# A two-layer hybrid with mixtures of experts on one core: all 32 experts loaded by index, all weight loads on one queue, no rank tables in the routing

## The chip, the cores and the metric

The kernel runs on one core of one Trainium2 chip. The metric is the device time of one execution in microseconds (us). A kernel's time is the median over runs. A profiled execution is shown with its own span.

## What is computed

Two layers over 1024 latent tokens (a batch of one, width 1024) and 256 context tokens. Layer 0 mixes with gated DeltaNet heads and a short convolution, layer 1 with windowed attention; after each comes a hierarchical mixture of experts. Layer 0's mixture works on all 1280 tokens, layer 1's on the 1024 latent ones. Everything is float32. The change touches the mixture only:

```python
def hier_moe(x, w_group, w_expert, w1, w3, w2):
    g_sel = argmax(x @ w_group)                   # one group of 4
    e_in = (x @ w_expert)[g_sel]                  # 8 experts of that group
    top_p, top_i = top_k(softmax(e_in), 2)
    weights = p_group * top_p / sum(top_p)
    expert_id = g_sel * 8 + top_i
    return expert_ffn_sorted(x, expert_id, weights, w1, w3, w2)

# assignments sorted by expert; every block of rows with its own expert's weights
    h = silu(xb @ w1[e]) * (xb @ w3[e])
    return h @ w2[e]
```

An expert has w1 and w3 (1024 x 512) and w2 (512 x 1024), 2048 KB (2.1 MB) each.

## The kernel before

The program is a row of stages, each a block in which all five engines run their own instruction stream and wait for each other by semaphores. A block ends when every engine has ended; then the next begins. The mixture `moe` is: a norm with the router's logits, `route`, `experts`, `combine`.

**`route`** runs on VectorE, instruction after instruction, each waiting for the one before. It counts tokens by expert and rounds each expert up to units of 64 rows. An assignment's row among them is its slot. GpSimd then writes the tokens' numbers to their slots by indirect DMAs (L1172). After the slots, VectorE goes on with a table: active experts in rank order (EXPERT), how many blocks are needed up to the last row of each rank (BLOCKS_UPTO), and for each block of 128 rows (two units) in which of the three buffers the weights of its two units lie, how many loads each buffer must have had by then, and which loads to make next (NEXT). The last instruction casts the table to integers (L1329). In layer 0 the same block also computes the modulation of layer 1 (`modulation`, its rows by VectorE at L232), which has no part in the mixture.

**`experts`** runs over the blocks of 128 rows. `w13` and `w2` are rings of three buffers, one expert each (RING = 3). TensorE does for block j, in this order: the transposes of the x of block j + 1 (L1439), those of the h of block j - 1 (L1445), up(j), which is 64 matmuls with w1 and w3 (L1463), and down(j - 1), which is 32 matmuls with w2 (L1483). ACT and VectorE copy and apply silu between them. GpSimd gathers the rows of x by an indirect DMA (L1412), ACT stores y (L1531).

The weights are loaded by two issuers:
- SP (`load13`, L1382) loads w1 and w3 of the next rank as soon as the buffer is free: w1 after the w1 half of up of the last block that used the buffer, w3 after its w3 half.
- ACT (`refill`, L1534 to L1549, then `load2`, L1538) issues w2 loads after it has copied and stored the y of a block: it reads from the table which ranks' buffers that block has freed.

up(j) waits for the loads into each w13 buffer that the table asks for, so for all experts up to its own second unit's; down(j) waits likewise for w2.

What the given inputs route follows from the reference alone. In layer 0 there are 56 units in 28 blocks, and their experts are (0,1) (2,3) (4,5) (6,7) (8,8) (9,10) (11,12) (12,13) (14,15) (16,17) (17,17) (17,17) (17,18) (18,18) (18,18) (19,19) (19,20) (20,21) (21,21) (22,22) (23,23) (23,23) (23,24) (24,25) (26,27) (28,28) (29,29) (30,31). In layer 1 there are 49 units in 25 blocks: (0,1) (2,2) (3,4) (4,5) (5,5) (5,5) (6,6) (6,7) (7,8) (9,10) (11,12) (13,14) (14,15) (15,16) (16,17) (17,18) (18,19) (20,20) (21,22) (23,24) (24,25) (25,26) (27,28) (29,30) (31,31). All 32 experts have tokens in both layers. Blocks are numbered from 0.

Of the kernel before, what the change touches and what calls it, by code (L numbers as in the profile page):

```python
# [21 lines left out]
P = 128  # L22
# [20 lines left out]
MAXP = ((2 * TOK + NE * (UNIT - 1)) // UNIT + 1) // 2  # L43
# [91 lines left out]
def ds(i, n):  # L135
    return bass.ds(i, n)
# [968 lines left out]
class Table:  # L1105


    BLOCKS, LAST, ACTIVE = 0, 1, 2
    EXPERT = 3
    BLOCKS_UPTO = EXPERT + NE  # L1110
    OF_BLOCK = BLOCKS_UPTO + NE
    PER = 2 + RING + 3
    NEXT = 2 + RING


    SIZE = OF_BLOCK + PER * (MAXP + 1)


def route(k, first, logits, slots, wts, table):
# [20 lines left out]
    active, rank_upto, rank = k.sb("active", [P, NE]), k.sb("active_upto", [P, NE]), k.sb("active_before", [P, NE])  # L1140
    far, last = k.sb("units_upto_if_active", [P, NE]), k.sb("last_rank", [P, 1])
    cmp, owner = k.sb("compare", [P, U, NE]), k.sb("owner_rank", [P, U])
    triple, rounds = k.sb("multiples_of_ring", [P, NE // RING + 1]), k.sb("rounds", [P, RING, U])
    last_unit, thresholds2 = k.sb("units_upto_rank", [P, NE]), k.sb("even_numbers", [P, MAXP])
    blocks_of = k.sb("blocks_of", [P, NE, MAXP])
    nxt = k.sb("next_rank", [P, MAXP + 1])
# [45 lines left out]
    def _(dve):  # L1192
# [59 lines left out]
        st.link(V.tensor_reduce(units[:], over[:], AX.X, ALU.add))  # L1252
        st.link(V.tensor_tensor_scan(incl[:], ones[:, 0:NE], units[:], 0.0, ALU.mult, ALU.add))
# [5 lines left out]
        for c in range(2):  # L1259
# [9 lines left out]
        R = slice(0, NE)  # L1269
        by_rank = ramp[:, R].unsqueeze(2).to_broadcast([P, NE, NE])  # L1270
        st.link(V.tensor_tensor(cmp[:, R], rank_upto[:].unsqueeze(1).to_broadcast([P, NE, NE]), by_rank, ALU.is_le))
        st.link(V.tensor_reduce(tf[:, Table.EXPERT:Table.EXPERT + NE], cmp[:, R], AX.X, ALU.add))
        st.link(V.tensor_scalar(tf[:, Table.EXPERT:Table.EXPERT + NE], tf[:, Table.EXPERT:Table.EXPERT + NE],
                                float(NE - 1), None, ALU.min))
        st.link(V.tensor_tensor(cmp[:, R], rank[:].unsqueeze(1).to_broadcast([P, NE, NE]), by_rank, ALU.is_le))
        st.link(V.tensor_tensor(cmp[:, R], cmp[:, R], units[:].unsqueeze(1).to_broadcast([P, NE, NE]), ALU.mult))
# [8 lines left out]
        st.link(V.tensor_copy(tf[:, Table.ACTIVE:Table.ACTIVE + 1], rank_upto[:, NE - 1:NE]))  # L1285

        st.link(V.tensor_scalar(far[:], active[:], -float(2 * U), float(2 * U), ALU.mult, ALU.add))
        st.link(V.tensor_tensor(far[:], far[:], incl[:], ALU.add))
        st.link(V.tensor_tensor(cmp[:], far[:].unsqueeze(1).to_broadcast([P, U, NE]),
                                ramp[:, 0:U].unsqueeze(2).to_broadcast([P, U, NE]), ALU.is_le))  # L1290
# [24 lines left out]
        st.link(V.tensor_scalar(last[:], rank_upto[:, NE - 1:NE], -float(RING), None, ALU.add))  # L1315
        st.link(V.tensor_scalar(last[:], last[:], 0.0, None, ALU.max))
        st.link(V.tensor_scalar(nxt[:], nxt[:], last[:, 0:1], None, ALU.min))
        st.link(V.tensor_scalar(per[:, :, Table.NEXT], nxt[:], float(RING), None, ALU.add))
        for u in range(2):

            if u:
                st.link(V.tensor_scalar(nxt[:], nxt[:], 1.0, None, ALU.add))
            st.link(V.tensor_scalar(triple[:], ramp[:, 1:NR + 1], float(RING), None, ALU.mult))
            st.link(V.tensor_tensor(cmp[:, 0:B, 0:NR], nxt[:].unsqueeze(2).to_broadcast([P, B, NR]),
                                    triple[:].unsqueeze(1).to_broadcast([P, B, NR]), ALU.is_ge))
            st.link(V.tensor_reduce(rounds[:, 0, 0:B], cmp[:, 0:B, 0:NR], AX.X, ALU.add))
            st.link(V.scalar_tensor_tensor(out=per[:, :, Table.NEXT + 1 + u], in0=rounds[:, 0, 0:B], scalar=-float(RING),
                                           in1=nxt[:], op0=ALU.mult, op1=ALU.add))
# [8 lines left out]
def experts(k, l, first, table):  # L1337
# [31 lines left out]
    @block.sync  # L1369
    def _(sp):  # L1370
        def entry(base, m, lo, hi):
            return sp.value_load(table[0:1, ds(m + base, 1)], min_val=lo, max_val=hi)

        def load13(m, r, wait=True):
            e = entry(Table.EXPERT, m, 0, NE - 1)
            used = entry(Table.BLOCKS_UPTO, m - RING, 1, MAXP) if wait else None

            for half, name in enumerate(("moe_w1", "moe_w3")):
                if wait:

                    sp.wait_ge((xw1_ready, up_ready)[half], primed(used))
                sp.dma_start(w13[:, r, half, :], dr[name][l, ds(e, 1)].rearrange("a (p j) n -> p (a j n)", p=P)).then_inc(w13_in[r], 16)  # L1382

        active = sp.value_load(table[0:1, Table.ACTIVE:Table.ACTIVE + 1], min_val=1, max_val=NE)
# [123 lines left out]
    @block.scalar  # L1508
    def _(act):
        def first(j):  # L1510

            act.wait_ge(xw1_ready, primed(j + 1))
            if not isinstance(j, int):
                act.wait_ge(h_turned, primed(j))
            nc.scalar.activation(h[:], k.bank[UP[0]][:], ACT.Silu).then_inc(silu_ready, 1)
            turned(j + 1)

        def turned(j):
            act.wait_ge(x_turned, primed(j + 1))
# [12 lines left out]

        def value(column, lo, hi):
            return act.value_load(table[0:1, ds(column, 1)], min_val=lo, max_val=hi)  # L1534

        def load2(rank, r):
            e = value(rank + Table.EXPERT, 0, NE - 1)
            act.dma_start(w2[:, r, :], dr["moe_w2"][l, ds(e, 1)].rearrange("a (p j) n -> p (a j n)", p=P)).then_inc(w2_in[r], 16)  # L1538
# [650 lines left out]
```

## Time and profile before

| | us |
|---|---|
| median of 3 runs | 4399.15 |
| lowest and highest run | 4390.29, 4408.07 |
| span of the profiled execution | 4404.1 |
| TensorE busy in the span | 3422.2 |
| first up to the last down of `experts`, layer 0 | 1755.8 to 2489.1 |
| the same, layer 1 | 3702.3 to 4338.9 |

The profiled execution is 5 us above the median. All times in rows are counted from the start of its span. Of TensorE's rows, PE is the matmuls and PEld the loads of the stationary operand. "q" behind an engine is its instruction sequencer, which waits, branches and issues DMAs. "<-" in brackets names what ended an engine's idle time.

### The profile page before, as it was taken

What the parts mean: (1) busy time and instruction counts of PE and PEld (TensorE: products, weight loads), DVE (VectorE), ACT (ScalarE), POOL (GpSimd) and SP (SyncE); (2) the same over time, 40 slices, a digit from 0 to 9 for tenths busy, and PEclk for the clock granted to TensorE, in tenths of its full rate; (3) what the DMA queues carried; (4) which work ended last, traced back from release to release, by engine and by line L of the source; (5) the groups of instructions that cost most, each with busy time, mean ns of one, the idle gap of its engine ahead of it and who ended that gap; (6) DMA issues with size and microseconds to landing.
All of it is one profiled execution on the core that took longest, in us unless ns stands there. A gap on an engine that the chain in (4) does not pass through costs nothing. (4 is left out here: it accounts for less than half of the span.)

```text
span 4404.1 us, 48676 instructions
## 1 busy us (share of the span) xinstructions
PE 3422.2 (78%) x15274; PEld 1825.7 (41%) x15275; DVE 1381.0 (31%) x2407; ACT 638.0 (14%) x1396; POOL 582.0 (13%) x522
## 2 busy tenths in 40 slices
PE   4899997999886952889998567677777953999983
PEld 0644443888883430233333133344444431333331
DVE  2223322555555162000111341155556142111014
ACT  1112211000002020000000121133334010000002
POOL 0000000333331111000000212111111111000002
PEclk7799998999997965899999778877778966999996
DMA  7311101011101067997567520120100017779994
GB/s 298 121 48 48 46 26 60 25 39 39 39 20 48 0 202 254 395 405 311 189 240 307 203 93 25 42 98 18 35 17 18 10 50 288 275 314 378 381 384 181
DMA packets 148767, 657.50 MB, mean 149 GB/s; under 512 B 25441, under 2 KB 63105, under 8 KB 117921
## 3 DMA queue, kind: packets, MB, share of 16 engines
q1 hardware_dynamic: 110688, 421.45, 25.3%
q10 hardware_dynamic: 17040, 162.24, 9.1%
q0 software_dynamic: 20912, 72.13, 4.7%
q8 instruction: 79, 1.29, 0.1%
q14 instruction: 48, 0.39, 0.0%
HBM read 586.41 MB, written 69.36 MB: 149 GB/s over the span
## 5 line engine op out<-in xcount | busy, mean ns | idle before, releaser
L1463 PE MATMUL bank<-w,xT 128*64 x3392 | 761.2, 608 | 52.6 <-DMA w<-in_moe_w 47.0
L502 PE MATMUL bank<-aT,w 128*128 128x512 f32 (+1 forms) x1344 | 500.7, 535 | 6.7 <-DVE short L661 5.9
L1463 PEld LDWEIGHTS bank<-w,xT 128*64 128x64 f32 x3392 | 244.9, 140 | 530.1 <-issue 525.4
L1483 PE MATMUL bank<-w,hT 128*64 (+1 forms) x1696 | 388.3, 611 | 64.6 <-issue 37.4
L502 PEld LDWEIGHTS bank<-aT,w 128*128 128x128 f32 x1344 | 266.4, 199 | 236.2 <-issue 220.0
L1580 DVE TENSOR_TENSOR h<-h,bank 128x512 f32<-128x512 f32 x53 | 36.5, 688 | 816.7 <-PE bank L1463 816.7
L1483 PEld LDWEIGHTS bank<-w,hT 128*64 128x64 f32 x1696 | 130.0, 140 | 321.7 <-issue 317.3
L1776 PE MATMUL bank<-at_w_in,aT 128*128 128x512 f32 x416 | 190.7, 620 | 3.5 <-PEq L116 3.5
L1439 PE MATMUL bank<-eye,x 128*128 128x128 f32 x440 | 65.5, 295 | 154.6 <-DMA x<-moe_x,idx_block 130.8
L377 PE MATMUL bank<-eye,a 128*128 128x128 f32 x304 | 68.1, 408 | 142.6 <-DVE a L361 132.1
L1975 PE MATMUL bank<-probsT,v_win 128*64 128x256 f32 x384 | 149.2, 566 | 36.4 <-DVE probsT L2077 36.4
L1961 PE MATMUL bank<-eye,probs 128*128 128x128 f32 x640 | 110.2, 314 | 72.2 <-POOL probs L2026 58.7
L1412 POOL DMA_INDIRECT x<-moe_x,idx_block x55 | 53.1, 965 | 853.1 <-PE bank L1439 851.4
L931 PE MATMUL bank<-T,AT 128*128 128x128 f32 x960 | 143.2, 301 | 12.3 <-DVE T L881 12.3
L2026 POOL TENSOR_TENSOR probs<-probs,den 128x640 f32<-128x640 f32 x64 | 80.3, 1254 | 498.2 <-DVE den L2060 498.2
L203 PE MATMUL bank<-ada_w,silu_c 128*2 128x512 f32 x384 | 78.4, 912 | 79.6 <-DMA ada_w<-in_ada_w 78.1
L1439 PEld LDWEIGHTS bank<-eye,x 128*128 128x128 f32 x440 | 55.7, 196 | 201.2 <-DMA x<-moe_x,idx_block 134.1
L931 PEld LDWEIGHTS bank<-T,AT 128*128 128x128 f32 x960 | 128.5, 209 | 23.2 <-DVE T L881 16.1
L931 PE MATMUL bank<-TT,A_T_off 128*128 128x128 f32 x960 | 126.7, 276 | 0.0
L1776 PEld LDWEIGHTS bank<-at_w_in,aT 128*128 128x128 f32 x416 | 82.8, 201 | 105.8 <-issue 105.8
L1961 PEld LDWEIGHTS bank<-eye,probs 128*128 128x128 f32 x640 | 78.6, 157 | 113.1 <-issue 84.1
L377 PEld LDWEIGHTS bank<-eye,a 128*128 128x128 f32 x304 | 58.0, 217 | 153.7 <-issue 115.3
(317 smaller groups left out, 4422.4 us busy)
## 6 DMA issues: line engine op xcount, KB each, us to landing
w<-in_moe_w SPq DMA_DIRECT2D x128, 2048.0 KB, 15.9
w<-in_moe_w ACTq DMA_DIRECT2D x64, 2048.0 KB
ada_w<-in_ada_w SPq DMA_DIRECT2D x48, 1024.0 KB, 22.4
moe_y<-y ACTq DMA_DIRECT2D x53, 512.0 KB
w<-in_ab_w_in SPq DMA_DIRECT2D x28, 512.0 KB, 3.7
moe_x<-a SPq DMA_DIRECT2D x18, 512.0 KB
moe_y<-zero POOLq DMA_DIRECT2D x1, 8192.0 KB, 26.2
at_w_in<-in_at_w_in SPq DMA_DIRECT2D x3, 2048.0 KB, 17.0
```

The lines of the kernel that those rows point to most:

```text
L203: mm = pe.matmul(bank(g, q)[32 * q:32 * q + 2, :], sc[:, j, :], w[:, j, q * NW:(q + 1) * NW], start=(j == 0), stop=(j == KC - 1))
L377: t = pe.transpose(k.bank[2 * u + c // 4][:, (c % 4) * P:(c % 4 + 1) * P], a[u][:, c * P:(c + 1) * P], k.eye[:])
L502: mm = pe.matmul(k.bank[3 * s + n][:, 0:width], w[j][:, c, :], aT[:, c, at:at + width], start=(c == 0), stop=(c == KC - 1))
L931: mm = pe.matmul(to[:, h, :], lhs[:, h, :], rhs[:, h, :], start=start, stop=stop)
L1412: pool.indirect_dma_start(x[:], None, dr["moe_x"], bass.IndirectOffsetOnAxis(ap=one[:, 0:1], axis=0)).then_inc(x_in, 16)
L1439: t = pe.transpose(k.bank[X[c // 4]][:, (c % 4) * P:(c % 4 + 1) * P], x[:, c:D:KC], k.eye[:])
L1463: mm = pe.matmul(k.bank[UP[half]][u * UNIT:(u + 1) * UNIT, :], xT[:, c, u * UNIT:(u + 1) * UNIT], w13[:, r if u else ds(buf[0], 1), half, ...
L1483: mm = pe.matmul(k.bank[Y[half]][u * UNIT:(u + 1) * UNIT, :], hT[:, c, u * UNIT:(u + 1) * UNIT], w2[:, r if u else ds(buf[0], 1), at:at + ...
L1776: mm = pe.matmul(k.bank[3 * s + g][:], aT[:, c, t * P:(t + 1) * P], w[:, c, g * 512:(g + 1) * 512], start=(c == 0), stop=(c == KC - 1))
L1961: mm = pe.transpose(k.bank[6 + f % 2][:, at:at + P], pr[m % 2][:, h, c * P:(c + 1) * P], k.eye[:])
L1975: mm = pe.matmul(to[HD * h:HD * h + HD, 0:2 * P], v, pt[g % 2][:, c, h, :, :], start=(c == 0), stop=(c == 4))
L2026: nc.gpsimd.tensor_tensor(pr[m % 2][:, 0, :], pr[m % 2][:, 0, :], small[m % 2]["den"][:, 0:1].to_broadcast([P, W + C]), ALU.mult).then_inc ...
```

## The change

The table loses the rank columns: EXPERT, ACTIVE and the three NEXT columns. Ranks are now the experts' own indices, and every expert gets at least one unit, with or without tokens (`ALU.max` with 1.0). SP loads all 32 experts in a written-out order, with w2 one place behind w1 and w3, and waits for the freed buffer by an entry of BLOCKS_UPTO. ACT loads no weights any more. MAXP is 36 with either formula.

```diff
-MAXP = ((2 * TOK + NE * (UNIT - 1)) // UNIT + 1) // 2
+MAXP = ((2 * TOK + NE * UNIT) // UNIT + 1) // 2
...
+def expert_at(n):
+    return n
...
         st.link(V.tensor_reduce(units[:], over[:], AX.X, ALU.add))
+        st.link(V.tensor_scalar(units[:], units[:], 1.0, None, ALU.max))
...
-        st.link(V.tensor_scalar(active[:], units[:], 1.0, None, ALU.min))
-        st.link(V.tensor_tensor_scan(rank_upto[:], ones[:, 0:NE], active[:], 0.0, ALU.mult, ALU.add))
-        st.link(V.tensor_tensor(rank[:], rank_upto[:], active[:], ALU.subtract))
...
-        st.link(V.tensor_reduce(last_unit[:], cmp[:, R], AX.X, ALU.add))
         st.link(V.tensor_scalar(thresholds2[:], ramp[:, 0:MAXP], 2.0, None, ALU.mult))
-        st.link(V.tensor_tensor(blocks_of[:], last_unit[:].unsqueeze(2).to_broadcast([P, NE, MAXP]),
+        st.link(V.tensor_tensor(blocks_of[:], incl[:].unsqueeze(2).to_broadcast([P, NE, MAXP]),
                                 thresholds2[:].unsqueeze(1).to_broadcast([P, NE, MAXP]), ALU.is_gt))
...
-        B = MAXP + 1
-        st.link(V.tensor_tensor(cmp[:, 0:B], tf[:, Table.BLOCKS_UPTO:Table.BLOCKS_UPTO + NE].unsqueeze(1).to_broadcast([P, B, NE]),
-                                ramp[:, 0:B].unsqueeze(2).to_broadcast([P, B, NE]), ALU.is_le))
-        st.link(V.tensor_reduce(nxt[:], cmp[:, 0:B], AX.X, ALU.add))
...
         st.link(V.tensor_copy(table[:], tf[:]))
...
     @block.sync
     def _(sp):
-        def entry(base, m, lo, hi):
-            return sp.value_load(table[0:1, ds(m + base, 1)], min_val=lo, max_val=hi)
-
-        def load13(m, r, wait=True):
-            e = entry(Table.EXPERT, m, 0, NE - 1)
-            used = entry(Table.BLOCKS_UPTO, m - RING, 1, MAXP) if wait else None
-
+        def used_upto(m):
+            at = Table.BLOCKS_UPTO + m
+            return sp.value_load(table[0:1, at:at + 1], min_val=1, max_val=MAXP)
+
+        def load13(m):
+            r, e = m % RING, expert_at(m)
+            used = used_upto(m - RING) if m >= RING else None
             for half, name in enumerate(("moe_w1", "moe_w3")):
-                if wait:
+                if m >= RING:
 
                     sp.wait_ge((xw1_ready, up_ready)[half], primed(used))
...
+        def load2(m):
+            if m >= RING:
+
+                sp.wait_ge(y_mm, primed(used_upto(m - RING)))
+            sp.dma_start(w2[:, m % RING, :], dr["moe_w2"][l, expert_at(m)].rearrange("(p j) n -> p (j n)", p=P)).then_inc(w2_in[m % RING], 16)
 
         sp.wait_ge(idx_in, 16)
-        load13(0, 0, wait=False)
+        load13(0)
         sp.wait_ge(x_in, 16)
-        for m in range(1, RING):
-            with sp.If(active > m):
-                load13(m, m, wait=False)
-        with sp.Fori(1, NE // RING + 1) as i:
-            for r in RR:
-                with sp.If(i * RING + r < active):
-                    load13(i * RING + r, r)
+        for m in range(1, NE):
+            load13(m)
+            load2(m - 1)
+        load2(NE - 1)
...
-        def refill(j):
-
-
-            per = j * Table.PER + Table.OF_BLOCK
-            lo, hi = value(per + Table.NEXT, RING, NE), value(per + (Table.PER + Table.NEXT), RING, NE)
-            for u in R2:
-                with act.If(lo + u < hi):
-                    buf = value(per + (Table.NEXT + 1 + u), 0, RING - 1)
-                    for r in RR:
-                        with act.If(buf == r):
-                            load2(lo + u, r)
-
-        active = value(Table.ACTIVE, 1, NE)
-        act.wait_ge(x_in, 16)
-        for m in RR:
-            with act.If(active > m):
-                load2(m, m)
         turned(0)
         first(0)
 
         def body(j):
             first(j)
             second(j - 1)
-            refill(j - 1)
```

The first place is SP's stream in the expert stage of layer 0. In the rows before, w_361 is `w13`; these are the first three experts and one turn of the loop over the ring:

```order
L1382 DMA w_361<-in_moe_w 128x4096 x2
L1390 COMPARE_AND_BRANCH
L1372 TENSOR_LOAD table
L1372 ISA x2
L1382 ISA
L1382 DMA w_361<-in_moe_w 128x4096 x2
...
L1394 COMPARE_AND_BRANCH
L1372 ISA
L1372 TENSOR_LOAD table
L1372 ISA x3
L1372 TENSOR_LOAD table
L1372 ISA x2
L1381 REGISTER_ALU
L1382 ISA
L1382 DMA w_361<-in_moe_w 128x4096 x2
```

In the changed kernel w_354 is `w13` and w_355 is `w2`; the stream starts so:

```order
L1346 DMA w_354<-in_moe_w 128x4096 x4
L1352 DMA w_355<-in_moe_w 128x4096
L1346 DMA w_354<-in_moe_w 128x4096 x2
L1352 DMA w_355<-in_moe_w 128x4096
L1337 TENSOR_LOAD table
L1337 ISA x2
L1345 REGISTER_ALU
L1346 DMA w_354<-in_moe_w 128x4096 x2
L1352 DMA w_355<-in_moe_w 128x4096
```

Each pair of w1 and w3 is now followed by one w2 in the same stream, and the branches are gone.

The second place is ACT's loop over the blocks. Before, the store of y is followed by table loads, branches and up to two loads of w2 (w_362):

```order
L1528 COPY y<-bank 128x512
L1531 ISA
L1531 DMA moe_y<-y 128x1024
L1534 ISA
L1534 TENSOR_LOAD table
L1534 ISA x3
L1534 TENSOR_LOAD table
L1534 ISA x2
L1546 COMPARE_AND_BRANCH
```

In the changed kernel the loop's body ends with the store:

```order
L1484 REGISTER_ALU
L1487 COPY xT<-bank 128x512
L1492 ISA
L1493 COPY y<-bank 128x512
L1496 ISA
L1496 DMA moe_y<-y 128x1024
```

## Rows read from the trace of the kernel before

**Rows 1.** The page: the span, and the busy time of each engine.

```profile
span 4404.1 us, 48676 instructions
...
PE 3422.2 (78%) x15274; PEld 1825.7 (41%) x15275; DVE 1381.0 (31%) x2407; ACT 638.0 (14%) x1396; POOL 582.0 (13%) x522
```

**Rows 2.** The page's costliest groups: the products up (L1463) and down (L1483).

```profile
L1463 PE MATMUL bank<-w,xT 128*64 x3392 | 761.2, 608 | 52.6 <-DMA w<-in_moe_w 47.0
...
L1483 PE MATMUL bank<-w,hT 128*64 (+1 forms) x1696 | 388.3, 611 | 64.6 <-issue 37.4
```

**Rows 3.** Windows: stretch, busy of each engine, then PEclk, DMA share, GB/s.

```profile
1755.00:2010.00 255.00, 211.40 (x940) 75.42 (x940) 23.36 (x35) 15.34 (x26) 10.30 (x18) 0.91 0.98 404
...
2010.00:2371.00 361.00, 341.15 (x1620) 124.41 (x1620) 39.40 (x59) 26.55 (x45) 16.22 (x29) 0.99 0.59 225
...
3712.00:3722.00 10.00, 7.62 (x41) 3.16 (x36) 1.98 (x3) 0.59 (x1) 0.60 (x2) 1.00 1.01 428
...
3702.00:3915.00 213.00, 199.86 (x942) 76.20 (x944) 22.66 (x34) 15.34 (x26) 9.37 (x17) 0.98 0.74 287
...
3915.00:3999.00 84.00, 71.76 (x320) 26.46 (x321) 8.02 (x12) 5.31 (x9) 3.44 (x6) 0.94 1.01 428
...
3999.00:4245.00 246.00, 228.76 (x1090) 85.36 (x1091) 27.41 (x41) 17.70 (x30) 12.44 (x21) 0.99 0.93 371
```

**Rows 4.** Timeline, TensorE, layer 0: start, length, what, idle time before.

```profile
1755.77 16.18 PE L1463 MATMUL bank<-w,xT 128*64 x64 [5.13 <-DMA w<-in_moe_w]
...
1782.15 16.64 PE L1463 MATMUL bank<-w,xT 128*64 x64 [7.03 <-DMA w<-in_moe_w]
...
1860.73 7.09 PE L1483 MATMUL bank<-w,hT 128*64 x32 [0.82 <-issue]
...
1867.89 1.13 PE L1439 MATMUL bank<-eye,x 128*128 128x128 f32 x8
...
1868.85 0.65 PE L1445 MATMUL bank<-eye,h 128*128 128x128 f32 x4
...
2010.01 13.95 PE L1463 MATMUL bank<-w,xT 128*64 x64 [2.07 <-DMA w<-in_moe_w]
...
2063.31 13.95 PE L1463 MATMUL bank<-w,xT 128*64 x64
...
2086.51 13.95 PE L1463 MATMUL bank<-w,xT 128*64 x64
```

**Rows 5.** Timeline, GpSimd, layer 0: waits for the first two gathers.

```profile
1729.63 0.18 POOL L1406 COPY idx_block<-idx 128x1 int32<-128x1 int32 x1 [10.95 <-DMA x<-moe_x,idx_block]
...
1748.79 0.18 POOL L1406 COPY idx_block<-idx 128x1 int32 x1 [15.38 <-DMA x<-moe_x,idx_block]
```

**Rows 6.** Timeline, ACT, layer 0: the copy of y and the next w2.

```profile
1836.90 0.59 ACT L1528 COPY y<-bank 128x512 f32<-128x512 f32 x1 [6.55 <-PE bank L1483]
...
1841.12 2.34 ACTq L1538 DMA_DIRECT2D w<-in_moe_w  x2
```

**Rows 7.** Timeline, VectorE, routing of layer 1.

```profile
3620.15 0.17 DVE L1265 TENSOR_SCALAR active<-units 128x32 f32<-128x32 f32 x1
...
3627.35 0.18 DVE L1278 TENSOR_SCALAR even_numbers<-ramp 128x36 f32<-128x36 f32 x1
...
3645.39 1.39 DVE L1312 TENSOR_TENSOR compare<-table_f,ramp 128x1184 f32<-128x1184 f32 x1
...
3652.74 0.35 DVE L1329 CAST table<-table_f 128x363 int32<-128x363 f32 x1
```

**Rows 8.** One line, L90, same stretch: the ends of the engines' blocks.

```profile
L90 POOLq DRAIN  x1: 1456/1456/1456, 3648.5 to 3648.5; - x1
```

**Rows 9.** Timeline, VectorE, layer 0: the routing's last row, the modulation's last.

```profile
1662.57 0.35 DVE L1329 CAST table<-table_f 128x363 int32<-128x363 f32 x1
...
1697.86 2.84 DVE L232 TENSOR_TENSOR rows<-bank,bias 2x512 f32<-2x512 f32 x4 [17.33 <-PE bank L203]
```

**Rows 10.** One tile, w, 1755 to 2010: durations min/median/max in ns.

```profile
L1463 PE MATMUL bank<-w,xT x576: 592/592/1116, 1755.8 to 1997.5; 128*64 x96, 128*64 128x512 f32 x96
```

More of the change, by code:

```diff
@@ L1105 @@
 class Table:
-    BLOCKS, LAST, ACTIVE = 0, 1, 2
-    EXPERT = 3
-    BLOCKS_UPTO = EXPERT + NE
+    BLOCKS, LAST = 0, 1
+    BLOCKS_UPTO = 2
     OF_BLOCK = BLOCKS_UPTO + NE
-    PER = 2 + RING + 3
-    NEXT = 2 + RING
+    PER = 2 + RING
     SIZE = OF_BLOCK + PER * (MAXP + 1)
+def expert_at(n):
+    return n
 def route(k, first, logits, slots, wts, table):
@@ L1139, in route @@
     over, thresholds = k.sb("over", [P, NE, MOST]), k.sb("thresholds", [P, MOST])
-    active, rank_upto, rank = k.sb("active", [P, NE]), k.sb("active_upto", [P, NE]), k.sb("active_before", [P, NE])
-    far, last = k.sb("units_upto_if_active", [P, NE]), k.sb("last_rank", [P, 1])
     cmp, owner = k.sb("compare", [P, U, NE]), k.sb("owner_rank", [P, U])
     triple, rounds = k.sb("multiples_of_ring", [P, NE // RING + 1]), k.sb("rounds", [P, RING, U])
-    last_unit, thresholds2 = k.sb("units_upto_rank", [P, NE]), k.sb("even_numbers", [P, MAXP])
+    thresholds2 = k.sb("even_numbers", [P, MAXP])
     blocks_of = k.sb("blocks_of", [P, NE, MAXP])
-    nxt = k.sb("next_rank", [P, MAXP + 1])
     ratio, inv = k.sb("ratio", [P, T]), k.sb("inv", [P, T])
@@ L1284, in _ @@
         st.link(V.tensor_scalar(tf[:, Table.LAST:Table.LAST + 1], tf[:, Table.BLOCKS:Table.BLOCKS + 1], -1.0, None, ALU.add))
[L1285 to L1289, printed above, removed]
+        st.link(V.tensor_tensor(cmp[:], incl[:].unsqueeze(1).to_broadcast([P, U, NE]),
                                 ramp[:, 0:U].unsqueeze(2).to_broadcast([P, U, NE]), ALU.is_le))
         st.link(V.tensor_reduce(owner[:], cmp[:], AX.X, ALU.add))
-        st.link(V.tensor_scalar(last[:], rank_upto[:, NE - 1:NE], -1.0, None, ALU.add))
-        st.link(V.tensor_scalar(owner[:], owner[:], last[:, 0:1], None, ALU.min))
+        st.link(V.tensor_scalar(owner[:], owner[:], float(NE - 1), None, ALU.min))
         NR = NE // RING + 1
@@ L1309, in _ @@
             st.link(V.tensor_copy(per[:, :, 2 + r], rounds[:, r, 1:U:2]))
-        B = MAXP + 1
-        st.link(V.tensor_tensor(cmp[:, 0:B], tf[:, Table.BLOCKS_UPTO:Table.BLOCKS_UPTO + NE].unsqueeze(1).to_broadcast([P, B, NE]),
-                                ramp[:, 0:B].unsqueeze(2).to_broadcast([P, B, NE]), ALU.is_le))
-        st.link(V.tensor_reduce(nxt[:], cmp[:, 0:B], AX.X, ALU.add))
[L1315 to L1328, printed above, removed]
         st.link(V.tensor_copy(table[:], tf[:]))
@@ L1370, in _ @@
     def _(sp):
-        def entry(base, m, lo, hi):
-            return sp.value_load(table[0:1, ds(m + base, 1)], min_val=lo, max_val=hi)
-        def load13(m, r, wait=True):
-            e = entry(Table.EXPERT, m, 0, NE - 1)
-            used = entry(Table.BLOCKS_UPTO, m - RING, 1, MAXP) if wait else None
+        def used_upto(m):
[4 more added lines that the diff above has]
+            used = used_upto(m - RING) if m >= RING else None
             for half, name in enumerate(("moe_w1", "moe_w3")):
-                if wait:
+                if m >= RING:
                     sp.wait_ge((xw1_ready, up_ready)[half], primed(used))
-                sp.dma_start(w13[:, r, half, :], dr[name][l, ds(e, 1)].rearrange("a (p j) n -> p (a j n)", p=P)).then_inc(w13_in[r], 16)
-        active = sp.value_load(table[0:1, Table.ACTIVE:Table.ACTIVE + 1], min_val=1, max_val=NE)
+                sp.dma_start(w13[:, r, half, :], dr[name][l, e].rearrange("(p j) n -> p (j n)", p=P)).then_inc(w13_in[r], 16)
+        def load2(m):
+            if m >= RING:
+                sp.wait_ge(y_mm, primed(used_upto(m - RING)))
+            sp.dma_start(w2[:, m % RING, :], dr["moe_w2"][l, expert_at(m)].rearrange("(p j) n -> p (j n)", p=P)).then_inc(w2_in[m % RING], 16)
         sp.wait_ge(idx_in, 16)
-        load13(0, 0, wait=False)
+        load13(0)
         sp.wait_ge(x_in, 16)
-        for m in range(1, RING):
-            with sp.If(active > m):
-                load13(m, m, wait=False)
-        with sp.Fori(1, NE // RING + 1) as i:
-            for r in RR:
-                with sp.If(i * RING + r < active):
-                    load13(i * RING + r, r)
+        for m in range(1, NE):
+            load13(m)
+            load2(m - 1)
+        load2(NE - 1)
     @block.gpsimd
@@ L1531, in second @@
             act.dma_start(dr["moe_y"][ds(j * P, P), :], y[:]).then_inc(y_stored, 16)
[L1533 to L1538, printed above, removed]
-        def refill(j):
-            per = j * Table.PER + Table.OF_BLOCK
-            lo, hi = value(per + Table.NEXT, RING, NE), value(per + (Table.PER + Table.NEXT), RING, NE)
-            for u in R2:
-                with act.If(lo + u < hi):
-                    buf = value(per + (Table.NEXT + 1 + u), 0, RING - 1)
-                    for r in RR:
-                        with act.If(buf == r):
-                            load2(lo + u, r)
-        active = value(Table.ACTIVE, 1, NE)
-        act.wait_ge(x_in, 16)
-        for m in RR:
-            with act.If(active > m):
-                load2(m, m)
         turned(0)
```

8 lines of the change are left out of this document (removed).

## The prediction

> **What bounds the kernel now.** I read the page first: 4404.1 us, TensorE busy 78% [rows 1]. Its groups put 761 + 388 us of TensorE into the products of the experts, so the two expert stages are about a third of the kernel; the change touches nothing else but the routing [rows 2].
>
> The windows show which limit holds where. From 1755 to 2010 in layer 0 the DMA engines are 98% busy at 404 GB/s and TensorE has 211 us of work in 255: transfers bound it. From 2010 to 2371 they are at 59% with TensorE at 341 of 361. Layer 1 changes the same way: 74% up to 3915, all of it from 3915 to 3999, 93% after that [rows 3]. The list of experts by block says why. An expert brings 6.29 MB, 15 us at 415 GB/s, and a block costs TensorE 23.4 us (13.95 up, 7.09 down, 1.13 + 0.65 of transposes, half a us of hops; the undisturbed ups of blocks 11 and 12 start 23.2 apart) [rows 4]. A block that brings two new experts needs 12.6 MB plus 1 MB of gather and store, 33 us; one that brings a single expert or none is bound by TensorE. Layer 0 has pairs in blocks 0 to 3, 5, 6, 8, 9, 24 and 27, layer 1 in blocks 0, 2, 9, 10, 11, 18, 19, 22 and 23.
>
> **The change: the loads.** The bytes stay the same: all 32 experts had tokens in both layers, and 64 pairs of w1/w3 and 64 w2 were already loaded. So no load is added and none of the removed conditions ever skipped one. What changes is who waits for whom. Before, ACT issued w2, and SP held only w1/w3, whose slot comes free at the end of up(b), b being the last block of the expert three back. Now SP issues, in one order, w13(m), w2(m-1), w13(m+1), w2(m), and an instruction of SP waits for all before it. w2(m-1) needs the slot of expert m-4, which comes free at the end of down of its last block, and TensorE runs down(b) only after up(b+1). So a w13 that was free to go waits behind a w2.
>
> Take two blocks with pairs, (2b, 2b+1) and (2b+2, 2b+3). w13(2b+3) is needed by up(b+1), and its slot is free at the end of up(b). Before, it went out at once, while down(b-1) ran. Now it stands behind w2(2b+1), whose slot is freed by down(b-1). The cycle is thus closed: end of down(b-1), then w2(2b+1) and w13(2b+3), then up(b+1), then down(b).
> - Three loads of 2.1 MB on SP's queue: 15.2 us at 415 GB/s. One queue alone reaches the full rate, 428 GB/s at 3712, where by the order of issues only SP has loads under way, against 404 from 1755 on with both, so the single queue costs no rate [rows 3]. I choose 415, between them.
> - The gather and the store of a block, 1.05 MB: 2.5 us, and 2 us for the landing (chosen; the first gather kept GpSimd waiting 10.95 us for 0.5 MB, so latencies are there) [rows 5].
> - up after an idle time: 16.7, from 16.18 and 16.64 against 13.95 without. The granted clock was 0.91 in the stretch with gaps, 0.99 in the one without [rows 3, 4]. Then down, 7.3.
> Together 43.7 us, against 33 by the bytes and against the 28.5 us that the blocks 1 to 9 took in the mean (1782.15 to 2010.01) [rows 4]. In between, the DMA engines stand idle while up and down run: the change turns a stretch bound by bytes into one bound by a loop.
>
> I walked both layers forward block by block by rules: FIFO per queue, the rate shared equally, slots freed as above, the prices as above. Layer 0, distances of up from block 1 to 9: 44, 44, 26, 35, 33, 26, 35, 44, together 288 against 228 in the trace. (26 is 16.7 + 7.3 + 2: everything has landed. 35 is four w13 halves and two w2, 30 us, released in one moment. 33 is up, then a whole w13 of 10 us, its landing and 1 MB.) Blocks 10 to 26 stay at 23.4; block 27 costs 5 more. Layer 1, against the trace: blocks 2 and 3 +10, 10 and 11 +27, 19 to 23 together +28.
>
> **What is gained.** w13(1) no longer shares the rate with three w2. up(0) waited for it until 1755.8; it now starts when x of block 1 has been gathered, which took 15.4 us beside two queues and 11.0 beside one [rows 5], so near 1746: -9 [rows 4]. Layer 1 the same. The release of a w2 is quicker: 4.2 us from the start of ACT's copy of y to the issue, because of its value loads and branches [rows 6], and SP now needs under one; this is in the walk. Block 1 of layer 1 needs one new expert and gains another 10.
>
> The walk gives +55 and +53 between its own two versions. Against the rows of the trace it gives +47 and +45: for the old kernel it ends 8 and 10 us too early, since it lacks some of the mutual slowing of queues. I take the middle, near +98 in all.
>
> **The routing.** After the cast of the slots VectorE built ranks. Those fall away: 3620.15 to 3627.35 (7.2 us), 3645.39 to 3652.74 (7.35), some 0.8 of small ones, and one maximum of 0.2 is added: VectorE ends 15 us earlier [rows 7]. But the block ends with its last engine. In layer 1 GpSimd is through with its scatters at 3650.0 (its drain of 1.46 from 3648.5 [rows 8]), VectorE at 3653.1: the gain is 3 us, not 15. If GpSimd still takes longer it is 0, and it can't be over 5, since its last scatters stay where they are. In layer 0 the modulation of layer 1 runs in the same block; its last rows are made at 1697.86, VectorE's routing ends at 1662.9: nothing there. If that cover were gone, it would be worth the 15 us of VectorE [rows 9]. ACT's removed table loads and branches lie between jobs of 0.6 us, in waits for TensorE, and are worth nothing but the quicker w2.
>
> Sum: 4404.1 - 3 + 98 = 4499 for the profiled execution, which lies 5 above the median shown; so **4495 us**.
>
> **A rule against it.** The windows show that SP's queue alone moves as much as two [rows 3]. The Trainium skill (DMA: Bandwidth & Descriptors, Issuing engines are not separate DMA queues) says that DMAs of all issuers run on the same 16 engines and that several issuers save only the time to issue. By that alone the move of w2 would cost nothing, and the first rival below would be the result. The rule speaks of engines, not of an issuer that waits; the trace agrees on the rate.
>
> **The rivals.**
> - Nothing is lost (0.07). The queue stays full because enough loads are released ahead: three slots cover down. Then the pair stretches stay at the byte limit, and what is left is -3, two starts of -9 and a few us of quicker w2: about 4375. For it: 98% busy DMA now, where lateness of issue would not matter if two loads stood queued. Against: in the loop above all three loads are released at one moment. It decides at a loop under 33 us.
> - Only part is lost (0.10): TensorE doesn't cool and transfers land quickly, so 7.1 + 16 + 14 = 37 us a loop, 4 over the bytes. With some seven such blocks in each layer that is +56, less 21 of starts and routing: 4430.
> - The clock makes it worse (0.08): after 18 us of idle up runs wholly at the lower level. The longest matmul shows 1116 ns against 592 for most [rows 10]; an up would take about 26 us. Ten more on each of some fourteen blocks: 4600 at most.
> - My forecast (0.75), own range 4450 to 4550, from the walk with 380 to 415 GB/s (+45 to +58 a layer) and the two ways of comparing it.
>
> **How the numbers follow.** The likeliest gives 4495. Its range with the upper half of the second rival gives 4435 to 4560. Half a per cent is 22 us, about what a measurement of this kernel can tell. Faster: most of the first rival, 0.05. Same: its rest and the low end of the second, 0.06. Slower: 0.89.
>
> **What would show it.** In the profile after: SP's waits for TensorE's down (w2) with w13 issued right behind them, and no w issue on ACT. TensorE's idle before up in the pair blocks grows from 3 to 7 us to 15 or more, released by the DMA of w; the distance of ups 1 to 9 in layer 0 goes from 228 to about 288. DMA share in that stretch falls from 98% to 75 or 80%. up(0) of layer 0 starts 29 us after the issue of the first gather, not 38. Blocks 10 to 23 of layer 0 stay at 23.4. VectorE's last routing instruction in layer 1 ends 15 us earlier, GpSimd's next load 3 to 4. I am wrong if the ups keep their distances in the pair stretch, or if another stage moves by more than a few us.

## Result: 2.15% slower, and the profile after

| | before | changed |
|---|---|---|
| median, us (4 runs each) | 4398.91 | 4503.8 |
| lowest and highest, us | 4390.29, 4408.07 | 4489.35, 4511.07 |
| span of the profiled execution, us | 4404.1 | 4509.4 |

The ratio is 1.0215, 95% interval 1.0172 to 1.0259. 4495 us had been forecast, with a range of 4435 to 4560.

The page of the changed kernel first: its span, the busy time of the engines, and the groups of up (now L1428) and down (L1448), to be held against [rows 1, 2].

```profile
span 4509.4 us, 46823 instructions
...
PE 3432.4 (76%) x15274; PEld 1832.4 (41%) x15275; DVE 1352.5 (30%) x2353; ACT 638.2 (14%) x1395; POOL 579.8 (13%) x522
...
L1428 PE MATMUL bank<-w,xT 128*64 x3392 | 774.8, 616 | 186.7 <-DMA w<-in_moe_w 175.0
...
L1448 PE MATMUL bank<-w,hT 128*64 (+1 forms) x1696 | 382.7, 603 | 39.4 <-issue 39.4
```

TensorE does the same work (3432 us busy against 3422). What grew is its idle time ahead of up: from 52.6 to 186.7 us, of which 175.0 ended with a load of weights [rows 2]. Ahead of down it fell from 64.6 to 39.4. These two together make +109 us, and the span grew by 105.3.

Which wait it is, the list of SP's waits in the expert stage of layer 0 shows (engine and line, what it waited for, us in total, times, longest). The first row is the kernel before, where SP waits for up (L1463) alone. In the changed kernel L1346 issues w1 and w3, L1352 issues w2.

```profile
SPq L1382 <- PE bank L1463: 600.3, 40, 67.8
```

```profile
SPq L1346 <- PE bank L1428: 353.5, 22, 57.8
SPq L1352 <- PE bank L1448: 338.3, 16, 40.4
```

Half of SP's waiting is now for down. What stands behind such a wait, SP's timeline shows:

```profile
1812.08 0.33 SPq L1352 DMA_DIRECT2D w<-in_moe_w  x1
1813.09 1.09 SPq L1346 DMA_DIRECT2D w<-in_moe_w  x2
1814.84 0.33 SPq L1352 DMA_DIRECT2D w<-in_moe_w  x1
1815.82 1.16 SPq L1346 DMA_DIRECT2D w<-in_moe_w  x2
1857.02 0.33 SPq L1352 DMA_DIRECT2D w<-in_moe_w  x1
1858.01 1.07 SPq L1346 DMA_DIRECT2D w<-in_moe_w  x2
```

And TensorE's timeline of the same stretch:

```profile
1781.33 16.87 PE L1428 MATMUL bank<-w,xT 128*64 x64 [9.42 <-DMA w<-in_moe_w]
1802.27 9.77 PE L1448 MATMUL bank<-w,hT 128*64 x32 [4.08 <-issue]
...
1833.44 16.41 PE L1428 MATMUL bank<-w,xT 128*64 x64 [19.60 <-DMA w<-in_moe_w]
1849.89 7.09 PE L1448 MATMUL bank<-w,hT 128*64 x32
...
2077.34 15.64 PE L1428 MATMUL bank<-w,xT 128*64 x64 [19.37 <-DMA w<-in_moe_w]
```

Read the two side by side. down(0) ends at 1812.04; 0.04 us later SP issues w2(3), and at 1813.09 the w1 and w3 of expert 5, whose slot had been free since up(1) ended at 1798.2. up(2) needs them and starts at 1833.44, after 19.60 us of idle time. down(1) ends at 1856.98, SP issues at 1857.02, and so on: the loop of the prediction.

The windows close it: from up of block 1 to up of block 9 in layer 0, and the same stretch that [rows 3] begins with.

```profile
1781.30:2077.30 296.00, 198.35 (x864) 69.96 (x864) 21.38 (x32) 14.16 (x24) 9.33 (x17) 0.82 0.79 326
...
1755.00:2010.00 255.00, 180.21 (x786) 63.14 (x782) 18.02 (x27) 12.40 (x21) 8.19 (x15) 0.84 0.80 331
```

The DMA engines fell from 98% and 404 GB/s to 80% and 331 GB/s; the granted clock from 0.91 to 0.84.

**Where the 105.3 us are.** The two expert stages, measured from the issue of the first gather to the end of the last down, went from 771.4 to 828.1 and from 674.8 to 724.5 us: +106.4. The rest cancels: the stages up to the first gather +4.7, those between the two expert stages -6.0 (of it -2.3 by the routing of layer 1, see below), the end +0.2. The same code ran there in both kernels but for the routing, and the stretch between the expert stages spans 1158 to 1191 us over the kernels of this study.

### The profile page after: what moved, and what is told of

It reads as the page before. It is cut to its first block and busy times, and to the rows that moved or that the text cites. A ratio compares the mean times of both kernels' runs of the same rounds, so it can differ in the third digit from the quotient of the medians.

```text
span 4509.4 us, 46823 instructions
## 1 busy us (share of the span) xinstructions
PE 3432.4 (76%) x15274; PEld 1832.4 (41%) x15275; DVE 1352.5 (30%) x2353; ACT 638.2 (14%) x1395; POOL 579.8 (13%) x522
## 5 line engine op out<-in xcount | busy, mean ns | idle before, releaser
L1428 PE MATMUL bank<-w,xT 128*64 x3392 | 774.8, 616 | 186.7 <-DMA w<-in_moe_w 175.0
L1428 PEld LDWEIGHTS bank<-w,xT 128*64 128x64 f32 x3392 | 247.3, 142 | 675.6 <-issue 671.3
L1448 PE MATMUL bank<-w,hT 128*64 (+1 forms) x1696 | 382.7, 603 | 39.4 <-issue 39.4
L1448 PEld LDWEIGHTS bank<-w,hT 128*64 128x64 f32 x1696 | 128.9, 139 | 292.1 <-issue 287.6
L1480 ACT ACTIVATE h<-bank 128x512 f32<-128x512 f32 x53 | 31.7, 597 | 696.9 <-PE bank L1428 696.9
```

The lines of the kernel that those rows point to most:

```text
L1428: mm = pe.matmul(k.bank[UP[half]][u * UNIT:(u + 1) * UNIT, :], xT[:, c, u * UNIT:(u + 1) * UNIT], w13[:, r if u else ds(buf[0], 1), half, ...
L1448: mm = pe.matmul(k.bank[Y[half]][u * UNIT:(u + 1) * UNIT, :], hT[:, c, u * UNIT:(u + 1) * UNIT], w2[:, r if u else ds(buf[0], 1), at:at + ...
```

## The experiments

Ratios are to the kernel before, run beside the other one on the same chip. Between the sets of runs the chips differ: before's median was 4399 us beside the changed kernel, 4421 beside the first "two places behind", "directly behind", "only w2 moved" and "SP static", 4414 beside the four rows after these, and 4432 beside "the same again" and "both of these". "Stage" is the time from the first gather's issue to the end of the last down, in one profiled execution. How far such a time can be read, the kernel that was profiled twice shows: 762.7 and 756.4 us in layer 0.

| kernel | ratio, 95% interval | stage, layer 0 | stage, layer 1 | up(1) to up(9), layer 0 | up(0) after gather, layers 0, 1 |
|---|---|---|---|---|---|
| before | 1 | 771.4 | 674.8 | 227.9 | 38.1, 38.2 |
| changed (w2 one place behind) | 1.0215 (1.0172 to 1.0259) | 828.1 | 724.5 | 296.0 | 30.7, 29.6 |
| w2 two places behind | 0.9933 (0.9908 to 0.9959) | 762.7 | 672.0 | 234.2 | 30.2, 30.1 |
| the same again | 0.9903 (0.9885 to 0.9920) | 756.4 | 672.2 | 230.6 | 30.5, 30.2 |
| w2 directly behind | one run, 4861.86 us | 989.7 | 914.3 | 405.1 | 31.5, 31.2 |
| before, only w2 moved to SP | 1.0208 (1.0160 to 1.0257) | 826.2 | 724.3 | 294.5 | 30.6, 31.2 |
| before, SP static | 1.0006 (0.9984 to 1.0029) | 769.8 | 666.9 | 226.8 | 35.1, 34.5 |
| wait kept, 29 w2 loads left out | 0.9936 (0.9908 to 0.9964) | 768.5 | 650.1 | 245.1 | 30.8, 30.2 |
| no wait, 29 w2 loads left out | 0.9758 (0.9727 to 0.9789) | 719.4 | 620.3 | 197.9 | 30.2, 30.1 |
| before, w2 starts later | 0.9988 (0.9970 to 1.0007) | 777.5 | 674.4 | 230.0 | 31.1, 30.6 |
| before, no rank tables | 0.9989 (0.9967 to 1.0011) | 768.8 | 672.6 | 226.9 | 34.9, 34.4 |
| both of these | 0.9945 (0.9924 to 0.9966) | 772.5 | 672.6 | 226.6 | 30.1, 30.0 |

### One place further back

```diff
         for m in range(1, NE):
             load13(m)
-            load2(m - 1)
-        load2(NE - 1)
+            if m >= 2:
+                load2(m - 2)
+        load2(NE - 2)
+        load2(NE - 1)
```

> The changed kernel with one thing moved: in SP's order w2 stands two places behind w1 and w3 (w13(m), w2(m-2)) instead of one. The loads, their count and the single queue stay. Theory A (a w13 that is free to go stands behind a w2 that waits for down): w13(2b+3) now goes out at the end of up(b), the loop over down is open, and pair blocks fall back to the byte limit of 25 to 34 us. The distance of the ups of blocks 1 to 9 in layer 0 goes from 296 back to 225 to 240 us, blocks 9 to 11 of layer 1 from 42 and 45 to about 33; total 4380 to 4400. Theory B (the single queue itself is the cost: w2 no longer interleaves with w13 on the DMA engines, or SP issues too slowly): nothing changes, 4504 +- 15.

Measured: 0.9933 (0.9908 to 0.9959). All bytes still go through SP's queue, with the same waits; only the order is another. w2(m-2) behind w13(m) waits for down of an expert that lies one further back, so its slot is free, or nearly, when SP comes to it. SP's waits in the stage of layer 0, with the same meaning as above, show it: 16 waits of 338.3 us for down became 13 of 102.2.

```profile
SPq L1346 <- PE bank L1430: 533.4, 40, 67.0
SPq L1352 <- PE bank L1450: 102.2, 13, 21.7
```

The window has the DMA engines full again, on one queue:

```profile
1755.00:2010.00 255.00, 202.30 (x924) 72.84 (x922) 23.36 (x35) 15.34 (x26) 10.30 (x18) 0.90 0.98 409
```

So neither the single queue nor the removed branches cost anything that the total shows. The place of w2 in the order does. A little of the wait is left: up(1) to up(9) took 234.2 and 230.6 us in the two profiles, against 227.9 before.

### Directly behind

```diff
         load13(0)
+        load2(0)
...
         for m in range(1, NE):
             load13(m)
-            load2(m - 1)
-        load2(NE - 1)
+            load2(m)
```

> The changed kernel with w2(m) directly behind w13(m) in SP's order. The suspected wait is doubled: down(b-1) now releases four loads, 12.6 MB, before the next up can start. Theory A: pair blocks take 7 + 33 + 17 = 57 to 59 us instead of 44, single ones in between 44; the ups of blocks 1 to 9 in layer 0 lie about 370 us apart; total near 4840. Theory B (single queue or bytes): unchanged, near 4504.

Measured: 4861.86 us in one run, a span of 4860.2; the stages cost +162 and +190 us over the changed kernel's. TensorE's timeline at the block whose idle time was 19.60:

```profile
1801.58 9.79 PE L1448 MATMUL bank<-w,hT 128*64 x32 [3.76 <-issue]
...
1847.11 16.08 PE L1428 MATMUL bank<-w,xT 128*64 x64 [33.91 <-DMA w<-in_moe_w]
1863.19 7.09 PE L1448 MATMUL bank<-w,hT 128*64 x32
```

From the end of down(0) at 1811.37 to up(2) it now takes 35.7 us, against 21.4 in the changed kernel: before up(2) can go, SP issues w2(3), w13(4), w2(4) and w13(5) after down(0), six loads or 12.6 MB instead of three. The difference of 14.3 us for 6.3 MB more is 440 GB/s, near the 428 of a full queue [rows 3]. The dose goes the way the loop says, and up(1) to up(9) came out at 405.1, longer than I had expected.

### Only w2 moved, tables and conditions kept

```diff
+        def load2(m):
+            e = entry(Table.EXPERT, m, 0, NE - 1)
+            if m >= RING:
+                sp.wait_ge(y_mm, primed(entry(Table.BLOCKS_UPTO, m - RING, 1, MAXP)))
...
-        for m in range(1, RING):
+        for m in range(1, NE):
             with sp.If(active > m):
-                load13(m, m, wait=False)
-        with sp.Fori(1, NE // RING + 1) as i:
...
+                load13(m, m % RING, wait=m >= RING)
+            with sp.If(active > m - 1):
+                load2(m - 1)
...
-            refill(j - 1)
```

> The kernel before with only the issuer of w2 changed: SP issues w13(m) and w2(m-1) in that order, still with index and condition read from the rank table; the routing with all its rank tables is kept, ACT's refill is gone. Theory A (the order on SP is all of the loss): the changed kernel's time plus the 2 us that the shorter routing gave, 4495 to 4515; SP's table loads of 0.6 us each may add up to 1 us to each of some 14 loops, 4520 at most. Theory C (a part of the loss comes from the static loads or the shorter tables): nearer to 4399 by over 15.

Measured: 1.0208 (1.0160 to 1.0257), the whole loss of the change, with stages of 826.2 and 724.3 us beside 828.1 and 724.5. The page's group of up reads as the changed kernel's:

```profile
L1469 PE MATMUL bank<-w,xT 128*64 x3392 | 773.3, 615 | 183.8 <-DMA w<-in_moe_w 173.5
```

### Only SP's conditions and table reads removed

```diff
-                sp.dma_start(w13[:, r, half, :], dr[name][l, ds(e, 1)].rearrange("a (p j) n -> p (a j n)", p=P)).then_inc(w13_in[r], 16)
+                sp.dma_start(w13[:, r, half, :], dr[name][l, m].rearrange("(p j) n -> p (j n)", p=P)).then_inc(w13_in[r], 16)
...
-        with sp.Fori(1, NE // RING + 1) as i:
-            for r in RR:
-                with sp.If(i * RING + r < active):
-                    load13(i * RING + r, r)
+        for m in range(1, NE):
+            load13(m)
```

> The kernel before with only SP's conditions and index reads removed: w1 and w3 of all 32 experts by constant index, written out; w2 stays on ACT with its refill, and the routing with all its tables is kept. Theory A: no effect, 4390 to 4408, since no condition ever skipped a load and SP waits for TensorE most of the time. Theory C (the written-out stream of SP costs by its instruction fetches, or the quicker SP changes how loads collide): over 20 us off 4399.

Measured: 1.0006 (0.9984 to 1.0029). up(0) starts 3.0 and 3.7 us earlier after the gather than before; the total shows nothing of it.

### The wait with and without its bytes

Both kernels are the changed one, with 29 of a layer's 32 w2 loads left out; in their place SP loads 16 KB, and the products down use a w2 that is out of date. They differ by one line:

```diff
         def load2(m):
             if m >= RING:
                 w = dr["moe_w2"][l, expert_at(m)].rearrange("(p j) n -> p (j n)", p=P)
-                sp.wait_ge(y_mm, primed(used_upto(m - RING)))
                 sp.dma_start(small[:, m, :], w[:, 0:32]).then_inc(small_in, 16)
                 return
```

> The changed kernel, but w2 is loaded for experts 0 to 2 only. In the place of each later w2 load SP keeps its wait for the product down and then loads 16 KB (32 columns) of it into a tile that nobody reads; the products down use the stale w2, so the output is not the reference's. 29 of 32 w2 loads of each layer are left out, a third of the bytes. A pair block then brings 8.4 MB plus 1 MB of gather and store, 23 us, as long as TensorE's own 23.4. My theory (the wait holds back the w1/w3 behind it): the loop of the pair blocks stays, shorter by one w2: 7.3 down + 10 of w1/w3 of one expert + 2 landing + 16.7 up = 36 us; layer 0 from up of block 1 to up of block 9 near 260 us although the bytes would allow 190. Against its pair without the wait about 95 us slower in all (45 to 50 a layer). Rival (the loss comes from the bytes on one queue, not from the wait): with a third of the bytes gone both kernels are TensorE-bound at about 23 to 25 us a block and end within 10 us of each other.

> The same kernel as the one with the wait only (29 of 32 w2 loads of each layer left out, 16 KB each in their place), but the 16 KB are loaded without a wait for the product down. Everything else, the order on SP's queue too, is the same. My theory: up of block 1 to up of block 9 of layer 0 at 190 to 215 us, the kernel about 95 us faster than its pair with the wait, no idle time of TensorE over 10 us before an up. Rival: within 10 us of its pair.

Measured: 4384.36 us with the wait, 4303.67 without, 80.7 us apart; the stages differ by 49.1 and 29.8, 78.9 together. I had said 95, 45 to 50 a layer: layer 0 is as expected, layer 1 lost less than I thought. up(1) to up(9) of layer 0 took 245.1 us with the wait, where I had said near 260, and 197.9 without, inside the 190 to 215. TensorE's timeline of both around block 2, first with the wait, then without:

```profile
1822.05 15.30 PE L1433 MATMUL bank<-w,xT 128*64 x64 [15.55 <-DMA w<-in_moe_w]
1837.26 7.09 PE L1453 MATMUL bank<-w,hT 128*64 x32
```

```profile
1810.01 13.95 PE L1432 MATMUL bank<-w,xT 128*64 x64
1823.88 7.09 PE L1452 MATMUL bank<-w,hT 128*64 x32
...
1833.11 13.95 PE L1432 MATMUL bank<-w,xT 128*64 x64
```

With the wait the idle time ahead of up is there although nothing is short of bandwidth: the DMA engines are 71% busy at 288 GB/s in the window below. Without it they are busier, 85%, because TensorE no longer stands.

```profile
1755.00:2010.00 255.00, 199.61 (x922) 72.52 (x918) 23.36 (x35) 15.34 (x26) 10.31 (x18) 0.91 0.71 288
```

```profile
1755.00:2010.00 255.00, 231.24 (x1088) 83.95 (x1086) 26.04 (x39) 17.69 (x30) 11.59 (x21) 0.97 0.85 341
```

That one `wait_ge` in SP's stream costs 79 us even with a third of the bytes gone, three quarters of what the change costs: the load at the head that waits and blocks those behind it is shown apart from the bytes.

### The start of a stage and the routing

In the kernel before, ACT's first three loads of w2 are held back until w1 and w3 of experts 0 and 1 have landed:

```diff
+        turned(0)
         active = value(Table.ACTIVE, 1, NE)
-        act.wait_ge(x_in, 16)
+        act.wait_ge(w13_in[1], primed(32))
         for m in RR:
             with act.If(active > m):
                 load2(m, m)
-        turned(0)
```

> The kernel before, but ACT issues its first three w2 loads only when w1 and w3 of experts 0 and 1 have landed (the whole output is computed). My theory for the start of a stage (w1/w3 of expert 1 shared the rate with three w2 loads, so up(0) waited): up(0) starts 29 to 31 us after the first gather's issue instead of 38 in both layers; the w2 loads end later but before down(0), so about 8 us a layer stay, 16 in all, ratio 0.996. Rival (the bytes are the limit in the first pair stretch, so what up(0) gains is given back by block 4 or 5): the ups of layer 0 from block 4 on stand where they stood, and the ratio is 0.999 to 1.001.

Measured: 0.9988 (0.9970 to 1.0007). The rival holds. up(0) starts 7.0 us sooner after the gather, but up(1) does not: it starts 65.1 us after it, 64.5 before [rows 4].

```profile
1752.29 15.95 PE L1463 MATMUL bank<-w,xT 128*64 x64 [2.56 <-DMA w<-in_moe_w]
...
1786.31 16.01 PE L1463 MATMUL bank<-w,xT 128*64 x64 [14.90 <-DMA w<-in_moe_w]
```

The 7 us come back as idle time ahead of up(1), 14.90 against 7.03. A transfer put off is not a transfer saved where bytes bound the stretch. The stage of layer 0 even came out 6.1 us longer, which is no more than two profiles of one kernel differ by.

Next, the kernel before without its rank tables. It also has SP's written-out loads of the kernel further up ("SP static"), and its up(0) starts where that one's does, at 34.9 us against 35.1.

```diff
-        st.link(V.tensor_scalar(active[:], units[:], 1.0, None, ALU.min))
-        st.link(V.tensor_tensor_scan(rank_upto[:], ones[:, 0:NE], active[:], 0.0, ALU.mult, ALU.add))
-        st.link(V.tensor_tensor(rank[:], rank_upto[:], active[:], ALU.subtract))
...
+        st.link(V.tensor_copy(tf[:, Table.EXPERT:Table.EXPERT + NE], ramp[:, 0:NE]))
```

> The kernel before, but the rank tables are removed as in the change (ranks are the experts' indices); SP loads w1 and w3 without conditions, and ACT keeps its refill of w2 with its NEXT table. The whole output is computed. My theory: VectorE ends some 7 us earlier in the routing (the NEXT table stays), GpSimd's scatters bound the block in layer 1 and the modulation in layer 0, so 2 us are gained in all: ratio 0.9985 to 1.0005, not to be told from no change. Rival (VectorE's chain bounds the routing): 7 us in each layer, ratio 0.997.

Measured: 0.9989 (0.9967 to 1.0011), no difference that can be told.

The last kernel of this group has both edits.

> Both edits to the kernel before at once: w2 of the first three experts held back until w1 and w3 of experts 0 and 1 have landed, and no rank tables. Each alone could not be told from no change (0.9988 and 0.9989). Theory: what up(0) gains at the start is given back in the pair stretch, which is bound by bytes, so nothing adds: 0.9975 to 1.0005; last down of layer 0 at 765 to 778 us after the first gather's issue. Rival: the gains add, below 0.997.

Measured: 0.9945 (0.9924 to 0.9966). By the ratio it is the rival, which had said below 0.997: the gains seem to add, or more than add, and I had not expected it. The profiled execution says the opposite: its stages, 772.5 and 672.6 us, are those of before within 2.2 us, with the last down of layer 0 inside the 765 to 778 of the theory. This stays open. On that chip the kernel before had the highest median of the study, 4431.9 us (4413.18 to 4436.72), while this kernel's own, 4410.5, is that of its two halves (4407.8 and 4409.4) on another chip.

### The best order once more

> The changed kernel with w2 two places behind w1 and w3, once more, beside the other candidate on one chip. Theory: its order keeps the single queue full and starts up(0) 30 us after the gather's issue, so it repeats 0.9933, within 0.991 to 0.996, and is the fastest version. Rival: the first ratio was partly the chip's, and it is 0.997 to 1.000, as the other candidate.

Measured: 0.9903 (0.9885 to 0.9920), 4388.65 us, 22 us below "both of these" on the same chip, below the interval of the first time and just below the 0.991 that I had given as the low end. The changed code with w2 two places behind is the fastest of the kernels here that compute the whole output, faster than the kernel before and than the changed one. Its two stages together are 11.5 us shorter than before's in the first profile and 17.6 in the second, which is 0.3 to 0.4%. The rest of the 0.7 and 1.0% is not in these stages, and I can't say where it is. The one profile of before is from another set of runs, and the stretch between the expert stages alone differs by 33 us between kernels (1158 to 1191), so single profiles can't place it.

```profile
1755.00:2010.00 255.00, 206.34 (x940) 74.03 (x938) 23.36 (x35) 15.33 (x26) 10.26 (x18) 0.91 0.99 415
```

Here one queue carries 415 GB/s with the DMA engines at 99%, against 404 and 98% for two [rows 3].

## Why the prediction was right, and where its sizes were off

**Bytes and conditions.** No load was added, none had been skipped. Right: SP issued 192 loads of w where SP and ACT had issued 128 and 64, and the kernel with only SP's conditions removed is at 1.0006.

**The sums.** The two stages together were forecast at +98 us and measured +106.4: layer 0 +56.7 (47 forecast), layer 1 +49.7 (45). Some sums of the prediction don't follow from its own terms. For layer 0 the terms shown are +60 from block 1 to 9, +5 for block 27 and -9 for the start, which is 56 and not 47; what the other -9 was, it doesn't say. A walk of layer 1 that gives +53 and ends 10 us too early would give +43, not 45. The eight distances add up to 287, the 33 us of block 6 are 31.2 by the terms named, and ten us on each of fourteen loops would have put the rival of the clock at 4635, not 4600.

**The loop.** Right, and nearly in size. It was priced at 7.3 + 19.7 + 16.7 = 43.7 us. The pair of blocks 2 and 3 took 44.2: 16.41 of up, 7.09 of down, 20.7 from its end to the next up. Block 9 took 45.2, blocks 10 and 11 of layer 1 42.5 and 45.4. up(1) to up(9) of layer 0 was 296.0 against 288 forecast and 227.9 before. The 8 us are in one place, as the other blocks' misses (block 6 took 29.4, not 33) nearly cancel: block 2 came 52.1 us after block 1, not 44, since down(0) began 4.08 us late and took 9.77 instead of 7.09, both in the rows above. The walk had priced the first down like the others.

**Layer 1.** The sum was right, +49.7 against +45, but two of its terms were not there. Block 1 was to gain 10 and blocks 2 and 3 to lose 10; measured, they moved by 0.4 together. The trace of before could have told: up(1) of layer 1 came 24.3 us after up(0) and up(2) 25.1 after that, near TensorE's own pace of 23.4, so there was nothing to gain. Nor was there anything to lose: up(2) and up(3) have no idle time ahead of them in the changed kernel either, for the loads that they need had landed in time. The two terms were of one size with opposite signs, so that the layer's sum came out right in spite of them was luck. The others held: blocks 10 and 11 +29.6 (27 forecast), blocks 19 to 23 +30.1 (28).

**Layer 0, smaller ones.** Block 27 cost +4.6 (5 forecast). Blocks 10 and 26 gained 5.3 and 8.1 us that I had not seen. Before, it was not their up that waited but the product down ahead of it, down(8) and down(24), for a w2 of ACT's:

```profile
2028.55 9.45 PE L1483 MATMUL bank<-w,hT 128*64 x32 [4.58 <-DMA w<-in_moe_w]
```

```profile
2415.74 8.71 PE L1483 MATMUL bank<-w,hT 128*64 x32 [6.77 <-DMA w<-in_moe_w]
```

In the changed kernel no down waits for a load: of the idle time ahead of down, 27.2 of 64.6 us ended with a load of w before, and nothing of the 39.4 after. The prediction had blocks 10 to 26 at 23.4 in both kernels. So layer 0 came out at +56.7 with 8 us more than forecast in the loop and 13.4 us of gain that wasn't in the sum; that these misses partly cancel was luck as well.

**The start.** -9 a layer was forecast; up(0) came 7.4 and 8.6 us sooner after the gather, and the second gather's wait fell from 15.38 [rows 5] to 10.94 us. In layer 1 the gain lasted to block 9 (up(9) 242.7 us after the gather against 250.8). Whether it is worth something depends on what follows: where bytes bound the next blocks, holding w2 back alone gave nothing (0.9988).

**The routing.** VectorE ended 15 us earlier, and the kernel got 2.3 of it, not 3. The first rows are VectorE's last one and GpSimd's next load of layer 1, the last is GpSimd's drain, with the start at its end.

```profile
3694.91 0.34 DVE L1293 CAST table<-table_f 128x219 int32<-128x219 f32 x1
```

```profile
3711.66 2.00 POOL L1365 DMA_DIRECT2D idx<-slot_token  x1 [9.37 <-POOLq L116]
```

```profile
L90 POOLq DRAIN  x1: 1451/1451/1451, 3707.3 to 3707.3; - x1
```

Before, VectorE's cast stood 4.2 us behind the start of GpSimd's drain [rows 7, 8]; now it stands 12.4 us ahead of it. From the last slots (VectorE at 3620.07 and 3677.72) to the load of idx it took 36.2 us before and 33.9 after. In layer 0 the cast came at 1653.79, with the first gather at 1722.40, behind the modulation as forecast [rows 9].

**The clock.** The stretch ran at 0.82, and an up behind 19.6 us of idle time took 16.4 us, not the 26 of the third rival. It stays at the price of an up behind 5 to 7 us. The windows show why: the granted clock is not at the lower level for the whole up. Here are three pieces of up(2) in layer 0, then the first down of layer 0 and the first down of layer 1:

```profile
1833.44:1837.44 4.00, 4.00 (x10) 1.25 (x12) 0.00 (x0) 0.00 (x0) 0.00 (x0) 0.50 1.01 430
1837.44:1841.44 4.00, 4.00 (x18) 1.23 (x16) 0.00 (x0) 0.00 (x0) 0.00 (x0) 0.88 0.99 422
1841.44:1849.85 8.41, 8.41 (x40) 2.56 (x36) 0.00 (x0) 0.60 (x1) 0.00 (x0) 1.00 0.52 224
...
1802.27:1812.04 9.77, 9.77 (x32) 2.90 (x32) 0.69 (x1) 0.00 (x0) 0.00 (x0) 0.72 0.00 0
...
3789.76:3797.02 7.26, 7.26 (x32) 4.14 (x32) 1.78 (x3) 0.37 (x1) 0.00 (x0) 1.00 0.15 63
```

The up starts at 0.50 (1.2 GHz) and ends at 1.00 (2.4 GHz). What the pause costs is the start at half the clock, so a longer pause costs no more. The slow first down is the same thing: it stands behind 4.08 us of idle time in layer 0 and runs at 0.72, and behind 0.32 us in layer 1, at 1.00. What down(0) of layer 0 waits for in these 4.08 us the profile doesn't show.

**The rivals.** "Nothing is lost" needed released loads ahead of the queue; SP's bursts within 0.04 us of down's end show that none stood there. It is what happens with w2 two places behind. "Only part is lost" needed a loop of 37 us; the loop took 44.2. The Trainium skill (DMA: Bandwidth & Descriptors, Issuing engines are not separate DMA queues) says that several issuers save only the time to issue. On the rate the traces agree, with 409 and 415 GB/s on one queue. On the time they don't: moving w2 to SP's stream alone cost 2.1% (1.0208), by SP's waits and not by the rate.

## What to carry to other kernels

Before loads are put on one issuer, list for each what frees its slot, and order the stream by when the slots come free, not by when the data is used: a load whose wait ends late holds back every load behind it, however free their slots are. The sign to look for is a burst of issues right behind the end of one product, with DMA share well below full and TensorE idle on a load; here, one place further back in the order turned +2.15% into -0.7 to -1.0%. A walk of the schedule must be held against the trace of before block by block, since its own errors look like gains and losses of the change.

## What the runs showed of the hardware

- The length of TensorE's pause hardly changed the price of the up behind it: 15.3 us behind 15.55, 16.41 behind 19.60, 16.08 behind 33.91, 13.95 without a pause. The granted clock stood at 0.50 at its start and at 1.00 at its end.
- The first down of layer 0's stage took 8.4 to 10.0 us in every kernel (9.77 in the changed one, at a granted clock of 0.72), that of layer 1's 7.1 to 7.3 (7.26 at 1.00), near the 7.09 of the later ones.
- Neither did the number of queues limit the rate: 404 GB/s with two and 409 to 415 with one, at 98 to 99% DMA share.
- The same program, before, had medians of 4399, 4414, 4421 and 4432 us in four sets of runs, the last three on three different chips, and the ratio of one kernel to it was 0.9933 on one and 0.9903 on another: a difference of a few tenths of a per cent between kernels of different sets is not to be read.
